# Weight splitting in a 256-token, two-block layer kernel: remainder kept in the raw slot, five raw and three rounded slots, waits by single k-tile, MLP loops written out

## What is computed

```python
def first_block(x, ...):
    h = rmsnorm(x, norm_mix_g); proj = h @ w_in                 # 2048 x 4096
    y_pool = rmsnorm(pool_mixer(u, pool_w, pool_scale), ...)
    y_attn = rmsnorm(dilated_attention(q, k, v, slopes), ...)
    x = x + concat([y_pool, y_attn]) @ w_out                    # 2048 x 2048
    x = x + square(relu(rmsnorm(x, norm_mlp_g) @ w_up)) @ w_down   # 2048 x 8192, 8192 x 2048
    return rmsnorm(x, norm_final_g)

def second_block(x, mem, ...):
    h = x + hybrid_mixer(rms_norm(x), w_in, ..., w_out)         # 2048 x 6160, gated delta rule,
                                                                # 4-tap and 31-tap convolutions, 2048 x 2048
    h = h + memory_cross_attention(...)                         # wq, wk, wv, wo: 2048 x 2048 each
    h = h + square(relu(rms_norm(h) @ w1)) @ w2                 # 2048 x 8192, 8192 x 2048
    return rms_norm(h, norm_final_g)
```

## Time and profile before

| | |
|---|---|
| three runs | 2709.28, 2711.86, 2712.61 us; median 2711.86 |
| span of the profiled execution, first to last instruction | 2708.4 us |
| mean granted TensorE clock | 0.992 of full |
| busy: PE, weight loads of PE, DVE, ACT, POOL | 2637.8, 2193.9, 1447.0, 1103.9, 40.1 us |
| transfers | 473.85 MB, 175 GB/s on average |

### The profile page before, as it was taken

The page is one execution under the profiler, slowest core; times in us unless marked ns, Lnnn a source line. Parts: engine busy times, 40 slices in busy tenths (PEclk is TensorE's granted clock), DMA queues, the critical chain, the costliest instruction groups (busy, mean ns, idle before and its releaser), DMA issues.

```text
span 2708.4 us, 31187 instructions
## 1 busy us (share of the span) xinstructions
PE 2637.8 (97%) x12404; PEld 2193.9 (81%) x12404; DVE 1447.0 (53%) x1243; ACT 1103.9 (41%) x956; POOL 40.1 (1%) x54
## 2 busy tenths in 40 slices
PE   7999999999999999999998999999999999999997
PEld 6888888888788887888887877887788888888886
DVE  4455545544455445667657796443455444455444
ACT  4444444433344334454225254443344433344333
POOL 0000000000000000001000000000000000000000
PEclk9999999999999999999999999999999999999999
DMA  7544655565555555655323355553555556555564
GB/s 271 192 151 134 200 175 191 180 199 189 181 180 189 190 192 156 232 173 170 109 78 125 109 186 172 177 180 115 167 187 184 187 188 198 189 187 186 187 191 151
DMA packets 121693, 473.85 MB, mean 175 GB/s; under 512 B 7280, under 2 KB 7920, under 8 KB 120144
## 3 DMA queue, kind: packets, MB, share of 16 engines
q1 hardware_dynamic: 119696, 460.29, 51.8%
q0 software_dynamic: 1856, 11.54, 1.2%
HBM read 467.61 MB, written 4.19 MB: 174 GB/s over the span
## 4 chain that ended last, share of the span: by engine, by line
PE 92%; ACT 3%; DVE 3%; issue 1%; DMA 0%; POOL 0%; SPq 0%; POOLq 0%; ACTq 0%; DVEq 0%
PE ps L634 28%; PE ps L635 28%; PE ps L638 28%; PE ps L848 2%; DVE weights_lo L1589 1%; ACT weights_hi L1187 1%; PE ps L683 1%; ACT stationary_hi L1202 1%; PE ps L737 1%; PE ps L612 1%; DVE conv_out L1784 1%; PE ps L1101 1%; PE ps L1117 1%; PE ps L1017 0%; PE ps L1008 0%
## 5 line engine op out<-in xcount | busy, mean ns | idle before, releaser
L1589 DVE TENSOR_TENSOR weights_lo<-weights_raw,weights_hi 128x2048 fp32r<-128x2048 f32 x434 | 994.2, 2291 | 1056.9 <-ACT weights_hi L1187 1056.9
L1187 ACT ACTIVATE weights_hi<-weights_raw 128x2048 fp32r<-128x2048 f32 x434 | 831.9, 1917 | 1340.1 <-PE ps L638 1340.1
L634 PE MATMUL ps<-weights_hi,stationary_hi 128*128 128x512 f32 x2432 | 965.1, 397 | 40.1 <-DVE weights_lo L1589 23.5
L635 PE MATMUL ps<-weights_lo,stationary_hi 128*128 128x512 f32 x2432 | 951.6, 391 | 0.0
L638 PE MATMUL ps<-weights_hi,stationary_lo 128*128 128x512 f32 x2432 | 752.9, 391 | 0.0
L634 PEld LDWEIGHTS ps<-weights_hi,stationary_hi 128*128 128x128 f32 x2432 | 460.2, 189 | 142.7 <-issue 38.6
L635 PEld LDWEIGHTS ps<-weights_lo,stationary_hi 128*128 128x128 f32 x2432 | 460.3, 189 | 96.5 <-issue 4.4
L638 PEld LDWEIGHTS ps<-weights_hi,stationary_lo 128*128 128x128 f32 x2432 | 458.8, 189 | 97.1
L634 PE MATMUL ps<-weights_hi,hidden_hi 128*128 128x512 f32 x1024 | 398.7, 389 | 0.0
L635 PE MATMUL ps<-weights_lo,hidden_hi 128*128 128x512 f32 x1024 | 398.4, 389 | 0.0
L638 PE MATMUL ps<-weights_hi,hidden_lo 128*128 128x512 f32 x1024 | 315.3, 389 | 0.0
(11 more groups left out here) (290 smaller groups left out, 988.6 us busy)
## 6 DMA issues: line engine op xcount, KB each, us to landing
weights_raw<-in_w SPq DMA_DIRECT2D x130, 1024.0 KB, 5.3
weights_raw<-in_w_in SPq DMA_DIRECT2D x80, 1024.0 KB, 5.4
weights_raw<-in_w_up SPq DMA_DIRECT2D x64, 1024.0 KB, 5.0
weights_raw<-in_w_down SPq DMA_DIRECT2D x64, 1024.0 KB, 5.6
weights_raw<-in_w_out SPq DMA_DIRECT2D x32, 1024.0 KB, 5.6
weights_raw<-in_wk SPq DMA_DIRECT2D x16, 1024.0 KB, 5.5
weights_raw<-in_wv SPq DMA_DIRECT2D x16, 1024.0 KB, 5.5
weights_raw<-in_wq SPq DMA_DIRECT2D x16, 1024.0 KB, 5.4
```

The lines of the kernel that those rows point to most:

```text
L634: pe.matmul(o, xh, WHI[:, slot, j, c * BANK:(c + 1) * BANK], start=first and j == 0, stop=False)
L635: pe.matmul(o, xh, WLO[:, slot, j, c * BANK:(c + 1) * BANK], start=False, stop=False)
L1187: act.activation(WHI[:, s % NSPLIT], RAW[:, s % NRAW], ACT.Copy).then_inc(hi_ready, 1)
L1589: dve.tensor_tensor(WLO[:, s % NSPLIT], RAW[:, s % NRAW], WHI[:, s % NSPLIT].bitcast(F32), ALU.subtract).then_inc(lo_ready, 1)
```

## The change

The remainder is written into the raw slot itself, tile by tile (`weights_lo` has the place of `weights_raw`). What this frees goes to a fifth raw slot and a third slot for the rounded part. A raw slot now holds what PE reads, so load s waits until PE has finished step s-5, and DVE no longer waits for PE. ACT and DVE split a step in two instructions of 1024 columns, one for each k-tile, and PE waits for `hi_ready` and `lo_ready` of each k-tile. The splits are still called two places ahead (`AHEAD`). The MLP halves are written out, and the two spare loads and their splits are gone. POOL's first transfers wait for the split of step 4, not 3.

```diff
-NRAW = 4
-NSPLIT = 2
+NRAW = 5
+NSPLIT = 3
+AHEAD = 2
...
-        WHI = at("weights_hi", [P, NSPLIT, STEP, COLS], 80, F32R)
-        WLO = at("weights_lo", [P, NSPLIT, STEP, COLS], 96, F32R)
+        WLO = at("weights_lo", [P, NRAW, STEP, COLS], 48, F32R)
+        WHI = at("weights_hi", [P, NSPLIT, STEP, COLS], 88, F32R)
...
-            def load(s, src, off=0):
+            def load(s, src):
                 if s >= NRAW:
-                    sp.wait_ge(hi_ready, s + off - NRAW + 1)
-                    sp.wait_ge(lo_ready, s + off - NRAW + 1)
+                    sp.wait_ge(w_used, s - NRAW + 1)
...
-                with sp.Fori(0, 2) as half:
-                    off = half * HALF_STEPS
+                for half in range(2):
+                    h0 = s0 + half * HALF_STEPS
...
-            for k in range(NSPLIT):
-                load(S_END + k, blocks(w1)[k, :, :, 0:COLS])
...
-            pool.wait_ge(hi_ready, NRAW)
+            pool.wait_ge(hi_ready, STEP * NRAW)
...
-            def step(s, hi, lo, k, group, first, last, off=0, between=None):
-                pe.wait_ge(hi_ready, s + off + 1)
-                pe.wait_ge(lo_ready, s + off + 1)
-                slot = s % NSPLIT
+            def step(s, hi, lo, k, group, first, last, between=None):
+                slot, low = s % NSPLIT, s % NRAW
                 for j in range(STEP):
+                    pe.wait_ge(hi_ready, STEP * s + j + 1)
+                    pe.wait_ge(lo_ready, STEP * s + j + 1)
...
-            def split(s, off=0):
-                act.wait_ge(raw_landed[s % NRAW], 16 * (s // NRAW + 1) + off * (16 // NRAW))
+            def split(s):
+                act.wait_ge(raw_landed[s % NRAW], 16 * (s // NRAW + 1))
                 if s >= NSPLIT:
-                    act.wait_ge(w_used, s + off - NSPLIT + 1)
-                act.activation(WHI[:, s % NSPLIT], RAW[:, s % NRAW], ACT.Copy).then_inc(hi_ready, 1)
+                    act.wait_ge(w_used, s - NSPLIT + 1)
+                for j in range(STEP):
+                    act.activation(WHI[:, s % NSPLIT, j], RAW[:, s % NRAW, j], ACT.Copy).then_inc(hi_ready, 1)
...
-            def split(s, off=0):
-                dve.wait_ge(hi_ready, s + off + 1)
-                if s >= NSPLIT:
-                    dve.wait_ge(w_used, s + off - NSPLIT + 1)
-                dve.tensor_tensor(WLO[:, s % NSPLIT], RAW[:, s % NRAW], WHI[:, s % NSPLIT].bitcast(F32), ALU.subtract).then_inc(lo_ready, 1)
+            def split(s):
+                for j in range(STEP):
+                    dve.wait_ge(hi_ready, STEP * s + j + 1)
+                    dve.tensor_tensor(WLO[:, s % NRAW, j], RAW[:, s % NRAW, j], WHI[:, s % NSPLIT, j].bitcast(F32), ALU.subtract).then_inc(lo_ready, 1)
```

More of the change, by code:

```diff
@@ L634, in step @@
                             pe.matmul(o, xh, WHI[:, slot, j, c * BANK:(c + 1) * BANK], start=first and j == 0, stop=False)
-                            pe.matmul(o, xh, WLO[:, slot, j, c * BANK:(c + 1) * BANK], start=False, stop=False)
+                            pe.matmul(o, xh, WLO[:, low, j, c * BANK:(c + 1) * BANK], start=False, stop=False)
                         for c in range(2):
@@ L669, in first_pass, with mlp @@
                 gemm_pass(s0, p, during, h, src)
-            def mlp(m, s0, p0, h):
+            def mlp(m, s_m, p_m, h):
                 pe.wait_ge(ht_lo, KT * h + KT // 2)
-                with pe.Fori(0, 2) as half:
-                    off, poff, aoff = half * HALF_STEPS, half * HALF_PASSES, half * 16
+                for half in range(2):
+                    s0, p0, a0 = s_m + half * HALF_STEPS, p_m + half * HALF_PASSES, 32 * m + 16 * half
                     def turn_hidden(p):
-                        pe.wait_ge(out0, p0 + p + 1 + poff)
-                        pe.wait_ge(out1, p0 + p + 1 + poff)
+                        pe.wait_ge(out0, p0 + p + 1)
+                        pe.wait_ge(out1, p0 + p + 1)
                         g = 4 * (p % 2)
@@ L1214, in ahead, with mlp @@
             def ahead(s0):
-                for k in range(NSPLIT):
+                for k in range(AHEAD):
                     split(s0 + k)
-            def mlp(m, s0, p0, norm):
+            def mlp(m, s_m, norm):
                 act.wait_ge(rstd_ready, norm + 1)
-                with act.Fori(0, 2) as half:
-                    off, roff = half * HALF_STEPS, half * 16
+                for half in range(2):
+                    s0, r0 = s_m + half * HALF_STEPS, 32 * m + 16 * half
                     def relu(p):
-                        act.wait_ge(w_used, s0 + (p + 1) * PS + off)
+                        act.wait_ge(w_used, s0 + (p + 1) * PS)
                         if p >= 1:
-                            act.wait_ge(r_turned, 32 * m + 4 * p + roff)
+                            act.wait_ge(r_turned, r0 + 4 * p)
                         g = 4 * (p % 2)
@@ L1345, in _ @@
                 split_turned(H_IN2, lambda k: G_IN2 + k, half, half)
-            for k in range(NSPLIT, PS):
+            for k in range(AHEAD, PS):
                 split(S_IN2 + k)
@@ L1626, in ahead_and_residual, with mlp @@
                 split(s_next + 1)
-            def mlp(m, s0, p0):
-                with dve.Fori(0, 2) as half:
-                    off, roff, hoff = half * HALF_STEPS, half * 16, half * 8
+            def mlp(m, s_m):
+                for half in range(2):
+                    s0, a0, h0 = s_m + half * HALF_STEPS, 32 * m + 16 * half, 16 * m + 8 * half
                     def square(p):
@@ L1740, in _ @@
             split_turned(H_MLP, lambda k: G_MLP + k, 1, 1)
-            mlp(0, S_MLP, P_MLP)
+            mlp(0, S_MLP)
             def final(n, dst):
```

76 lines of the change are left out of this document (39 added, 37 removed).

## The result

| | kernel before | changed kernel |
|---|---|---|
| median, us (range, runs) | 2712.18 (2709.28 to 2712.61, 4) | 2687.51 (2684.68 to 2690.02, 4) |
| ratio of the changed kernel, 95% interval | | 0.9913 (0.9899 to 0.9926) |
| profiled execution / its span, us | | 2687.99 / 2686.2 |

The change makes the kernel 24.7 us (0.87%) faster; the forecast was 2688.0 us. The number was right, in part by luck.

The account below looks back on a forecast made before the run. PE was taken as the bound, busy 2637.8 of 2708.4 us, with gains only in its holes. Terms 6.9 + 11.4 + 2.9 + 1.7 + 1.0 = 23.9 us gave a 2684.5 us span, 2688.0 us median; range 2680 to 2699.

Parts of the forecast that it names:

- The loops written out: At the MLP loop seams: PE's holes and the clock fall behind the first seam all go, 6.9 us gained.
- Single k-tiles: PE gets its first work of a step sooner, so waits for the remainder shrink or go; 11.4 us over five stretches.
- 30 to 300: Stretch 30 to 300 us: five PE waits for the remainder, the longest 1.2 us, all gone; 4.3 us gained.
- 1040 to 1100: Stretch 1040 to 1100 us: two PE waits, the longest 0.5 us, gone; 0.9 us gained.
- The start: Stretch 12 to 30 us: DVE's first tile can end at 16.87 instead of 18.62; 1.7 us gained.
- 1640 to 1700: Stretch 1640 to 1700 us: three waits, 4.2 us, of which DVE's own lateness keeps 0.4; 3.8 us gained.
- 1700 to 1800: Stretch 1700 to 1800 us: one PE wait, gone; 0.7 us gained.
- The convolution: 1440 to 1475 and 1551 to 1584 us, where DVE is late: its tiles come sooner; 2.9 and 1.7 us gained.
- What more instructions cost: DVE 35 to 65 us more, ACT some 90, hidden under PE; 0.5 us where DVE is late, already counted.
- Slots and waits: Extra slots, changed load waits and PE's 432 mid-step waits: no effect, at most a small loss at the start.
- The end: Kernel's end: without the unused rounding and split the final work comes sooner, between 0.6 and 1.2; 1.0 us taken.
- Given back: Rival, chance 0.16: PE comes earlier and meets the next late engine, so only 6 to 18 us gained, 2694 to 2706.

Follow-up runs that it names:

- e8: The changed kernel again, unchanged, beside three others on one chip; 2687.52 us, ratio 0.9917 to the kernel before.
- e9: The kernel before, PE taking its two fulfilled waits of a step a second time ahead of the second k-tile; 2706.13 us, ratio 0.9987.
- e10: The kernel before with four more fulfilled waits a step on PE ahead of the second k-tile; 2705.49 us, ratio 0.9983.
- e6: The kernel before with only rounding, subtraction and PE's waits by single k-tiles, its loops and slots kept; 2688.92 us, ratio 0.9924.
- e3: The changed kernel, PE waiting for both k-tiles of a step before its first matmul, splits still single; 2689.0 us, ratio 0.9928.
- e1: The kernel before with only its two MLP loops written out and no loads after the last step; 2703.24 us, ratio 0.9972.
- e2: The changed kernel with rounding, subtraction and PE's waits by whole steps of two k-tiles again; 2699.07 us, ratio 0.9962.
- e4: The changed kernel with 2 rounded slots in place of 3; 2686.18 us, ratio 0.9916.
- e7: The changed kernel with 4 raw slots in place of 5; 2688.0 us, ratio 0.9921.

## Why the prediction was right

Part of how close it came is luck. The span of the profiled execution was forecast at 2684.5 us and is 2686.2, 1.7 more. To get the median of the runs the prediction added 3.5, the distance between the median and the profiled span before; after, that distance is 1.3 (2687.51 - 2686.2). The two errors cancel. Against the kernel before run beside it, e8 gains 21.7 us (2709.19 - 2687.52), not 24.7.

**The loops written out, 6.9 us.** The place and the size held (7.0 by the matmuls), the cause did not. The step said of the hole behind the first seam, "All of it goes", and charged it to the loop. e9 and e10 keep the loop and lose the hole; e6 too. It went with each of the three additions to PE's code, and a transfer of code lies in it. What the jump cost in every kernel that kept it is 0.2 to 1.0 us of idle time; the rest, 3.4 us and the clock behind it, 1.6 by the matmuls side by side (1.8 in the forecast), went by edits that had nothing to do with the loop. With the k-tiles in, writing the loops out is worth some 1.4 us by the medians (e6 against e8, the slots included), no more than the runs scatter.

**Single k-tiles, 11.4 us.** The waits went much as forecast (6 times and 10.5 us are left, about 5 and 9 to 10 were expected), but four of the five terms were mis-sized; together they measured 9.2 (0.0 + 5.7 + 2.2 + 0.5 + 0.8).
- *30 to 300*, 4.3 forecast, 5.7 measured. The five waits gave 4.8. PE also came out of attention's short pieces sooner, 0.1 to 0.5 us at a time, in places where its wait had been put down to something else or none was drawn.
- *1040 to 1100*, 0.9 forecast. The holes gave 1.0 as said; the rest of the 2.2 is a clock that stayed low for 3.4 us instead of 6.8. That can't be put to the change: e9 and e10, with the splits and waits for them of before, have 3.4 there too, and e3, with single k-tiles, has 6.8.
- *The start*, 1.7 forecast. PE's first step did come 1.84 us sooner, counted from the landing of x. But x landed 0.95 later in this execution, and the clock rose later in the matmul stream; nothing was left. The landing scatters over 2.1 us (e1 to e10), with four slots and with five. It was an error to forecast a single execution's start within 2 us.
- *1640 to 1700*, 3.8 forecast, and the three waits gave 0.74 + 1.05 + 1.91 = 3.7. Then the clock took 3.1 back: at 1.2 GHz PE does in 6.8 us half of what it would. The prediction had thought of a fall of the clock behind a hole alone, and there was none.
- *1700 to 1800*, 0.7 forecast, 0.8 measured.

Why single k-tiles help was half wrong too: the prediction spoke of PE's first work coming sooner. By e3 that is half of it at most; the rest is that ACT and DVE overlap within a step.

**The convolution, 2.9 + 1.7 us.** Measured 3.1 and 1.75. The step that followed the chain from ACT to DVE through the stretch, instead of adding up waits, was worth its length. Its reason for the 0.88 us at 1567.28, the third slot, holds where the splits are wide (e2 against e1), but single k-tiles take the wait away without it (e4).

**What more instructions cost.** Hidden, as said, and less than forecast. DVE's split time is 1017.3 us for 864 against 994.2 for 434, 23 us more where 35 were the least (27.7 for the same 432 steps: 0.064 us a step), and 1.2 more in 130 us of MLP. On ACT it is 865.2 against 831.9, 33 us more where 90 were forecast: two roundings in a row overlap as well. The page of the Trainium skill that the prediction named, "VectorE: DVE Perf Modes", section "The TRN2 errata", gives its formula for a float32 addition; one subtraction of 1024 columns, 1.220 us, fits it, and the extra 0.064 us for a second one is less than the 0.16 of the estimate. At the tightest place DVE came to 49.28 of 50 where 48.9 was forecast, and PE was short of nothing.

**Slots and waits, nothing.** Right for the changed kernel (e4, e7, e9, e10; e6 for both slots at once). With wide splits the slots would have been worth some 4 us (e1, e2), which the prediction did not see. In some places slots and small tiles are two ways to the same gain (the 0.88 us; 1040 to 1100, where e2 has no wait either); in 30 to 300 only small tiles help (e2 waits 3.4 us there, the kernel before 3.5).

**The end, 1.0 us.** Measured 1.1.

**The rivals.** "Given back" happened once, in 1640 to 1700, through the clock and not through a late engine. The mid-step waits cost nothing, tested twice. DVE did not become the bound. Written-out code did not starve a queue. The errors of the terms lie on both sides and mostly cancelled: 22.2 us between the profiled executions where 23.9 were summed.

What stays open: why the granted clock falls at 1654, with PE drawn as covered. It does so in e1 too, where only the loops are written out, and in e6, where they are not, but not in the kernel before, e9 and e10. So it belongs to no one part of the change; what decides it was not tried. Open, too, is where PE's share in the gain of the single k-tiles lies between e3's medians and its waits.

## What to carry to other kernels

When PE is the bound and stands only at the joints, list its holes by what ends them, and ask of each whether the work behind it could start on half of its data, or whether PE has something else to do first; the second brought 16 us here, the first some 14 (e6's 20.3 less the 5.9 that the matmuls side by side give at its two seams), and the slots nothing on top. Parts of a change that close the same hole don't add up: run each alone in the old kernel and alone left out of the new one. An idle time that no semaphore explains may come and go with the amount of code: add code that does nothing, and see whether it stays.

## What the runs showed of the hardware that was not expected

- A loop's jump back cost PE 0.2 to 1.0 us, and in one layout of the code another 3.2 us six matmuls later, with one transfer of code in the hole. Two more fulfilled waits a step removed that hole and made the kernel 3.3 us faster (0.9987, 0.9978 to 0.9996).
- The granted clock fell to 1.2 GHz for 6.8 us in 1654.4 to 1661.2 of the changed kernel though PE was drawn as covered for 14.00 of 14.00 us ahead of it, its last work being matmuls of 2 columns; in e8, the same kernel again, within two matmuls of the same place.
- A fulfilled wait in mid-step costs PE nothing that can be seen, with 1728 of them added (e10, 2705.49 us against 2709.41).
